# Second-half query and key projections by seven block products each, in a two-layer fp32 decoder step

## The chip, the cores and the metric

The kernel runs on one core of one Trainium2 chip. The metric is the device time of one execution in microseconds. All arithmetic is fp32. Engines are named as in the profile: PE is TensorE's matmul, PEld its load of stationary operands, DVE VectorE, ACT ScalarE, POOL GpSimd, SP the queue that issues most loads.

## The reference

Two layers run over 512 prompt tokens and 8 sample tokens of width 1024. Cut to the part that matters:

```python
def project_mixers(h, w_in_l, pos):
    z = h @ w_in_l
    qa, ka, va, qi, ki, wi, qb, kb, vb, gb = jnp.split(z, splits, axis=-1)
    qa = rope(qa...); ka = rope(ka...); qi = rope(qi...); ki = rope(ki...)
    qb = rope(qb.reshape(B, T, H_B, HEAD_DIM), pos)
    kb = rope(kb.reshape(B, T, H_B, HEAD_DIM), pos) * (HEAD_DIM ** -0.5)

def trunk_layer(x, l, pos, ...):
    h = rmsnorm(x, g_mix_pre[l])
    qa, ka, va, qi, ki, wi, qb, kb, vb, gb = project_mixers(h, w_in[l], pos)
    a = mixer_a(qa, ka, va, qi, ki, wi)                       # top-k sparse softmax attention
    b, S = retention_mixer(qb, kb, vb, gb, s0, g_ret_l)       # "second half"
    x = x + rmsnorm(concat([a, b]) @ w_out[l], g_mix_post[l])
    f = square(relu(rmsnorm(x, g_ffn_pre[l]) @ w_up[l])) @ w_down[l]
    x = x + rmsnorm(f, g_ffn_post[l])
    return x, ka, va, ki, S
```

## The kernel before

The engines run programs written out by hand, one instruction stream each, that meet at semaphores; each engine works strictly in the order of its stream. A layer is a chain of stages on PE. The input projection is cut into eight chunks of 512 columns: chunk 0 the indexer, 1 and 2 query and key of the first half, 3 its values, 4 and 5 query and key of the second half (qb, kb), 6 the gate, 7 the values of the second half. Then come 16 output products and the feed-forward part, whose large products already use seven block products for eight (`product`, L1063).

`project` (L702) makes one chunk: for each of four tiles of 128 tokens, eight matmuls (k = 0 to 7) with a 128x128 block of tokens as the stationary and 512 columns of weights as the moving operand, and a fifth tile for the 8 sample tokens (L724, 32 small matmuls). An fp32 matmul is two instructions in the trace. After each k a hook, `between`, may place other work. Two PSUM banks alternate from tile to tile, so a tile can start when the tile two before it has been read (`bank_taken`). ACT reads a finished tile, scaled by a per-token factor, into one of three buffers `raw` (`evacuate`, L1224), and DVE applies the rotary embedding from there into `zr` (`rope`, L1614 to L1620, four instructions).

Under chunks 4, 5 and 6 the sparse attention of 32 (query block, head) pairs runs as a pipeline of steps. `head_steps` (L90) spreads steps 0 to 35 over the tiles by their cost. Step i of `attend` is, on PE, for even i the scores of pairs i and i+1 (L863), for i of 3 and more the transposes of the probabilities of pair i-3 (L873), and for odd i of 5 and more the products with the values of pairs i-5 and i-4 (L850), placed before the transposes. On DVE it is for even i two `masked_max` (L1657 adds the mask and takes the maximum, L1660 multiplies it by -1/8), then for pair i-1 the reciprocal of the sum (L1672) and the scaling of the probabilities by it (L1675). On ACT it is the copy of the transposed pair i-3 (L1259) and the exponential of pair i (L1264). A pair is 128 to 512 wide, by query block. Between the steps DVE has ropes and, in chunk 6, the gate's `sigmoid` (L1684, two reciprocals L1688, L1692), which waits for ACT's exponential of the gate (L1232). At the end of a query block ACT also copies its output (`block_out`, L1271). At the start of chunk 4 PE also replicates the sample's values (L887) and transposes its probabilities (L893), and multiplies these with cached values in two groups (L905); the buffers of the second group's cache are those that earlier products have to be through with.

POOL has next to nothing to do from the copies of the new sample keys (L2167, chunk 3) to the gate's gains (L2173, chunk 6).

## Time and profile before

| | us |
|---|---|
| median of three runs | 1585.12 |
| lowest and highest | 1582.35, 1586.71 |
| the profiled execution's own time | 1587.15 |
| its span | 1585.4 |
| busy PE / DVE / ACT / POOL | 1559.8 / 829.9 / 440.6 / 419.4 |
| granted PE clock, mean share of full | 0.999 |

The two layers are nearly alike; chunk 4 of the first starts at 139.3 us and its chunk 6 ends at 281 us, and the second layer's are some 787 us later. A timeline row gives the start of a run of like instructions and its length up to the modelled end of the last, which overlaps the next row; so what a run costs is the distance from its start to the next start.

### The profile page before, as it was taken

To read this page: it belongs to the slowest core of one execution; us is meant where nothing else is said; L and a number is where in the kernel's file an instruction comes from. 1 tells how busy PE (TensorE), PEld (TensorE's weight loads), DVE (VectorE), ACT (ScalarE), POOL (GpSimd) and SP (SyncE) were. 2 spreads that over 40 slices of the span, in tenths; PEclk is the share of its full clock that TensorE was granted. 3 is DMA by queue.
4 is the path that set the end of the run, shared out by engine and by line. 5 is a ranking of instruction groups with operands and counts; after the bars stand their busy time and mean duration, and the time that the engine had idled before them with its cause. 6 is when DMAs were issued, how large, how long until landed. Compare 5 with 4: busy or idle time off the path is not lost.

```text
span 1585.4 us, 21168 instructions
## 1 busy us (share of the span) xinstructions
PE 1559.8 (98%) x7774; PEld 1117.7 (70%) x7774; DVE 829.9 (52%) x1752; ACT 440.6 (28%) x1021; POOL 419.4 (26%) x330
## 2 busy tenths in 40 slices
PE   8999999999999999999999999999999999999998
PEld 5444445588888888888844444456888888888887
DVE  4699567855653003332467985688466520133334
ACT  5222245224421002310252213452253310032101
POOL 0000001013654324444320000010236534233461
PEclk9999999999999999999999999999999999999999
DMA  6426310123331222212223262110233321222211
GB/s 209 132 69 214 133 54 11 45 85 107 133 133 54 107 103 84 80 57 103 87 78 107 80 222 99 54 54 3 84 134 133 107 106 54 106 96 91 80 53 54
DMA packets 52807, 150.35 MB, mean 95 GB/s; under 512 B 8250, under 2 KB 29506, under 8 KB 39394
## 3 DMA queue, kind: packets, MB, share of 16 engines
q1 hardware_dynamic: 45218, 140.65, 25.6%
q10 hardware_dynamic: 7488, 8.36, 1.6%
q8 instruction: 62, 1.02, 0.2%
q14 instruction: 39, 0.32, 0.1%
HBM read 139.79 MB, written 9.02 MB: 94 GB/s over the span
## 4 chain that ended last, share of the span: by engine, by line
PE 81%; DVE 12%; ACT 2%; DMA 2%; SPq 1%; issue 1%; POOL 1%; DVEq 0%; ACTq 0%; POOLq 0%
PE ps L1063 46%; PE ps L720 17%; PE ps L1001 7%; DVE arena L1643 2%; DVE top L1641 2%; PE ps L873 2%; PE ps L863 1%; PE ps L850 1%; DVE x_feat L1798 1%; PE ps L724 1%; PE ps L959 1%; DVE arena L1875 1%; DVE s_sb L1796 1%; ACT arena L1224 1%; DMA arena<-in_cache_v 1%
## 5 line engine op out<-in xcount | busy, mean ns | idle before, releaser
L720 PE MATMUL ps<-wring,h_feat 128*128 128x512 f32 (+1 forms) x960 | 436.0, 591 | 3.9 <-ACT h_feat L1186 2.3
L720 PEld LDWEIGHTS ps<-wring,h_feat 128*128 128x128 f32 x960 | 171.1, 191 | 176.2 <-issue 161.1
L1063 PE MATMUL ps<-arena,wring 128*128 128x256 f32 (+1 forms) x1280 | 285.8, 382 | 0.3 <-DVE arena L1882 0.3
L1063 PEld LDWEIGHTS ps<-arena,wring 128*128 128x128 f32 x1280 | 243.0, 190 | 37.7 <-DVE arena L1882 1.1
L1063 PE MATMUL ps<-h_feat,wring 128*128 128x256 f32 (+1 forms) x768 | 176.6, 381 | 0.0
L2149 POOL TENSOR_TENSOR wring<-wring,arena 128x512 f32<-128x512 f32 (+1 forms) x48 | 78.8, 1642 | 345.1 <-PE ps L1063 321.8
L1063 PEld LDWEIGHTS ps<-h_feat,wring 128*128 128x128 f32 x768 | 145.9, 190 | 21.6
L1063 PE MATMUL ps<-mix,wring 128*128 128x256 f32 (+1 forms) x512 | 120.2, 383 | 0.7 <-DVE p_sb L1856 0.7
L1063 PE MATMUL ps<-arena 128*128 128x264 f32 x512 | 119.2, 386 | 0.0
L1001 PE MATMUL ps<-mix,wring 128*128 128x256 f32 (+1 forms) x512 | 115.0, 383 | 0.8 <-ACT mix L1285 0.8
L1224 ACT ACTIVATE arena<-ps,rtok 128x512 f32<-128x512 f32 (+3 forms) x128 | 65.5, 512 | 174.0 <-PE ps L720 165.3
L1063 PEld LDWEIGHTS ps<-arena 128*128 128x128 f32 x512 | 97.3, 190 | 16.4
L1063 PEld LDWEIGHTS ps<-mix,wring 128*128 128x128 f32 x512 | 97.2, 190 | 16.2 <-DVE p_sb L1856 1.1
L1001 PEld LDWEIGHTS ps<-mix,wring 128*128 128x128 f32 x512 | 96.5, 190 | 15.5 <-issue 1.2
L2132 POOL TENSOR_TENSOR pt_sb<-pt_sb 128x256 f32<-128x256 f32 (+1 forms) x94 | 72.9, 776 | 126.2 <-ACT pt_sb L1160 122.7
L2173 POOL TENSOR_TENSOR arena<-arena,gret 128x512 f32<-128x512 f32 (+1 forms) x10 | 14.6, 1460 | 289.2 <-ACT arena L1232 289.2
L1326 ACT ACTIVATE arena<-arena 128x264 f32<-128x264 f32 (+1 forms) x96 | 40.4, 421 | 182.1 <-DVE arena L1882 131.6
L2149 POOL TENSOR_TENSOR arena<-wring 128x512 f32<-128x512 f32 (+1 forms) x48 | 79.4, 1655 | 35.0 <-DMA wring<-in_w_all 12.1
L2149 POOL TENSOR_TENSOR wring<-wring 128x512 f32<-128x512 f32 (+1 forms) x48 | 79.7, 1661 | 3.8
L2149 POOL TENSOR_TENSOR arena<-arena,wring 128x512 f32<-128x512 f32 (+1 forms) x48 | 79.3, 1653 | 3.8
L2167 POOL COPY arena<-kTs 128x4 f32<-128x4 f32 x16 | 3.5, 218 | 228.3 <-ACT kTs L1386 219.5
L1063 PE MATMUL ps<-mix,arena 128*128 128x264 f32 x256 | 62.2, 386 | 0.0
(225 smaller groups left out, 1804.6 us busy)
## 6 DMA issues: line engine op xcount, KB each, us to landing
wring<-in_w_all SPq DMA_DIRECT2D x108, 1024.0 KB, 5.0
arena<-in_cache_k SPq DMA_DIRECT2D x32, 256.0 KB, 5.2
arena<-in_cache_v SPq DMA_DIRECT2D x32, 256.0 KB, 4.3
o_k_out<-arena ACTq DMA_DIRECT2D x2, 1024.0 KB
o_v_out<-arena ACTq DMA_DIRECT2D x2, 1024.0 KB
arena<-in_state SPq DMA_DIRECT2D x2, 1024.0 KB, 4.8
o_rets_out<-arena ACTq DMA_DIRECT2D x2, 1024.0 KB, 9.5
wring<-in_w_idx SPq DMA_DIRECT2D x3, 648.0 KB, 5.7
```

The costliest lines, as they stand in the source:

```text
L720: last = mm(ps[:, proj_bank(n), 0:width], h_feat[:, k, token_cols(t)], wt, start=(k == 0), stop=(k == KD - 1))
L724: last = mm(ps[32 * g:32 * g + NB, proj_bank(n), 0:c1 - c0], h_feat[:, k, SEQ:TOK], wt[:, c0:c1], start=(k == 0), stop=(k == KD - 1))
L850: last = mm(ps[e * HD:(e + 1) * HD, 6 + b % 2, (h // 2) * P:(h // 2 + 1) * P], v_tok[:, m, (h + e) * HD:(h + e + 1) * HD], pt_sb[e][:, m * ...
L873: last = nc.tensor.transpose(ps[:, 2 + j % 2, m * P:(m + 1) * P], p_sb[j % P_SLOTS][:, m * P:(m + 1) * P], idn[:])
L1001: last = mm(ps[:, item_bank(n), 0:span(h)], wring[u % SLOTS][:, (m % 2 * KD + k) * P:(m % 2 * KD + k + 1) * P], mix[:, k, HALVES[h]], star ...
L1063: last = mm(out, a[:, j, :], b, start=(opens(n) and j == 0), stop=(j == nk - 1), skip_group_check=True)
L1224: nc.scalar.activation(dst[:, c0:c1], ps[rr, proj_bank(n), 0:c1 - c0], ACT.Copy, scale=rtok[rr, sc, t:t + 1]).then_inc(done, 1)
L1326: nc.scalar.activation(f, f, ACT.Relu).then_inc(act_step, 1)
L1641: v.max(t8, w).then_inc(dve_step, 1)
L1643: v.match_replace(w, t8, w, MARK).then_inc(dve_step, 1)
L2132: nc.gpsimd.tensor_tensor(ssum[:, hc], ssum[:, hc], sqr[added % 2][:, 0:span(h)], ALU.add).then_inc(sq_used, 1)
L2149: nc.gpsimd.tensor_tensor(dst, in0, in1, op).then_inc(s_ready, 1)
```

## The change

Chunks 4 and 5 (`BLOCKED`) are no longer made by tiles. Tokens, input features and output columns are each halved; the eight block products that this gives (256 tokens, 512 features, 256 columns each) become seven, numbered 1 to 7, of sums and differences of blocks. `project_blocks` runs them in the order 1, sample tile (0), 2, 6, 5, 7, 3, 4 (`BLOCKS`). One block product is eight matmuls with 256 moving columns, four for each of two token tiles. Products 2, 7 and 3 accumulate into the bank that 1, 6 and 5 left, once these have been read out.

POOL makes the operands: per layer four sums of token blocks (`input_sum`) and four sums of weight blocks per chunk (`chunk_sum`), each 128x1024: the token sums 1 to 3, chunk 4's sums 1 and 2, token sum 4, the other sums of chunk 4, and chunk 5's. ACT reads product 1 (`take_p1`) and 5 (`take_p5`) unscaled, product 2's bank scaled (`take_first`, two instructions of 256), and scales the other three quarters in SBUF once DVE has summed them (`scale_quad`, two instructions each). DVE adds five sums of 512 per chunk (`chunk_u2`, `_u3`, `_c22`, `_c12`, `_c21`); its ropes then work in place and follow later: four of chunk 5's five now stand in chunk 6.

Apart from that, the scaling of all 32 pairs' probabilities moves from DVE to ACT (in step i, the exponential of pair i and then the scaling of pair i-1, which waits for DVE's reciprocal), and `masked_max` takes the minimum of values already multiplied by -1/8, so that L1660 goes. `head_steps` spreads the steps by the new costs: steps 0 to 3 stand in products 3 and 4 of chunk 4, 4 and 5 in product 1 of chunk 5, 6 at the end of its sample tile, 7 and 8 in product 2, 9 and 10 in 6, 11 and 12 in 5, 13 and 14 in 7, 15 and 16 in 3, 17 and 18 in 4, then four to each tile of chunk 6 after k = 1, 3, 5, 7 (19 to 34), and 35 in its sample tile. Before, chunk 6 began with step 20 and its second tile with step 24.

The diff, cut to its core:

```diff
 FT = 16
-ATT_FROM = 4 * TILES + 3
+BLOCKED = (4, 5)
+BLOCKS = (1, 0, 2, 6, 5, 7, 3, 4)
 ATT_STEPS = NT * NH + 4
...
+            def project_blocks(c, between):
+
+                q = BLOCKED.index(c)
+                for i, n in enumerate(BLOCKS):
+                    if i < 2:
+                        unit_here(2 * c + i)
+                    taken, value = bank_taken(c, i)
+                    pe.wait_ge(taken, past(taken) + value)
+                    if n == 6:
+                        pe.wait_ge(chunk_sums, past(chunk_sums) + 4 * q + 2)
+                        pe.wait_ge(in_sums, past(in_sums) + 2)
+                    if n == 7:
+                        pe.wait_ge(chunk_sums, past(chunk_sums) + 4 * q + 3)
+                        pe.wait_ge(in_sums, past(in_sums) + 3)
+                    if n == 3:
+                        pe.wait_ge(chunk_sums, past(chunk_sums) + 4 * q + 4)
+                    if n == 4:
+                        pe.wait_ge(in_sums, past(in_sums) + 4)
+                    for k in range(KD):
+                        t, j = divmod(k, 4)
+                        low, high = slice(t * P, (t + 1) * P), slice((t + 2) * P, (t + 3) * P)
+                        if n == 0:
+                            last = sample_tile(c, i, k)
+                        else:
+                            a = {1: chunk_block(c, "11"), 2: chunk_block(c, "12"), 3: chunk_block(c, "12"),
+                                 4: chunk_block(c, "22"), 5: cs1, 6: cs2, 7: chunk_block(c, "21")}[n][:, j, :]
+                            b = {1: h_feat[:, j, low], 2: h_feat[:, 4 + j, low], 3: h_feat[:, 4 + j, high], 4: in4[:, j, low],
+                                 5: in1[:, j, low], 6: in2[:, j, low], 7: in3[:, j, low]}[n]
+                            last = mm(product_bank(c, n)[:, t, :], b, a, start=(opens(n) and k == 0), stop=(j == 3),
+                                      skip_group_check=True)
...
+            def take_p1(c):
+
+                if c == 5:
+                    act.wait_ge(out_k, past(out_k) + 32)
+                act.wait_ge(proj_done, past(proj_done) + product_at(c, 1))
+                nc.scalar.activation(quad_of(c, "21"), product_bank(c, 1), ACT.Copy).then_inc(proj_p1, 1)
+                act.wait_ge(proj_p1, up(proj_p1))
...
+            def take_first(c):
+
+                act.wait_ge(proj_done, past(proj_done) + product_at(c, 2))
+                scaled(c, "11", product_bank(c, 2), proj_c11)
+
+            def scale_quad(c, which, summed):
+
+                act.wait_ge(summed, past(summed) + BLOCKED.index(c) + 1)
+                scaled(c, which, quad_of(c, which), proj_scaled)
...
+            def beside(c, i):
+
+                if (c, i) == (4, 7):
+                    scale_quad(4, "22", proj_c22)
+                if (c, i) == (5, 0):
+                    scale_quad(4, "12", proj_c12)
+                if (c, i) == (5, 1):
+                    take_p1(5)
+                    act.wait_ge(as_mm, past(as_mm) + 1)
+                    nc.scalar.activation(mix[:, 0:4, SEQ:TOK], ps[:, 7, 0:4 * NB].rearrange("p (h b) -> p h b", b=NB), ACT.Copy).then_inc(as_read, 1)
+                    act.wait_ge(as_read, up(as_read))
+                    scale_quad(4, "21", proj_c21)
+                if (c, i) == (5, 2):
+                    evacuate(5, 1)
+                if (c, i) == (5, 3):
+                    take_first(5)
+                if (c, i) == (5, 5):
+                    take_p5(5)
+                if (c, i) == (5, 7):
+                    scale_quad(5, "22", proj_c22)
+                if (c, i) == (6, 0):
+                    scale_quad(5, "12", proj_c12)
+                if (c, i) == (6, 1):
+                    evacuate(6, 0)
+                    scale_quad(5, "21", proj_c21)
+                if c == 6 and i > 1:
+                    evacuate(6, i - 1)
...
                     act.wait_ge(att_read, past(att_read) + i + 1)
                     nc.scalar.activation(p_sb[i % P_SLOTS][:, 0:n], s_sb[i % 2][:, 0:n], ACT.Exp,
-                                         bias=neg_mx[:, i % 2:i % 2 + 1], scale=ATT_SCALE,
+                                         bias=neg_mx[:, i % 2:i % 2 + 1], scale=-1.0,
                                          accum_out=rsum[:, i % P_SLOTS:i % P_SLOTS + 1]).then_inc(p_exp, 1)
                     act.wait_ge(p_exp, up(p_exp))
+                if 1 <= i <= NT * NH:
+                    j = i - 1
+                    p = p_sb[j % P_SLOTS][:, 0:(j // NH + 1) * P]
+                    act.wait_ge(r_ready, past(r_ready) + j + 1)
+                    nc.scalar.activation(p, p, ACT.Copy, scale=rinv[:, j % 2:j % 2 + 1]).then_inc(p_ready, 1)
+                    act.wait_ge(p_ready, up(p_ready))
...
                 v.tensor_tensor_reduce(out=s_sb[c][:, 0:n], in0=ps[:, 4 + c, 0:n], in1=masks[b],
-                                       scale=1.0, scalar=-3e38, op0=ALU.add, op1=ALU.max, accum_out=mx[:, c:c + 1]).then_inc(dve_step, 1)
-                dve.wait_ge(dve_step, up(dve_step))
-                v.tensor_scalar(neg_mx[:, c:c + 1], mx[:, c:c + 1], -ATT_SCALE, None, ALU.mult).then_inc(att_read, 1)
+                                       scale=-ATT_SCALE, scalar=3e38, op0=ALU.add, op1=ALU.min,
+                                       accum_out=neg_mx[:, c:c + 1]).then_inc(att_read, 1)
...
-                    n, c = (j // NH + 1) * P, j % 2
                     dve.wait_ge(p_exp, past(p_exp) + j + 1)
-                    v.reciprocal(rinv[:, c:c + 1], rsum[:, j % P_SLOTS:j % P_SLOTS + 1]).then_inc(dve_step, 1)
-                    dve.wait_ge(dve_step, up(dve_step))
-                    p = p_sb[j % P_SLOTS][:, 0:n]
-                    v.tensor_scalar(p, p, rinv[:, c:c + 1], None, ALU.mult).then_inc(p_ready, 1)
-                    dve.wait_ge(p_ready, up(p_ready))
+                    v.reciprocal(rinv[:, j % 2:j % 2 + 1], rsum[:, j % P_SLOTS:j % P_SLOTS + 1]).then_inc(r_ready, 1)
+                    dve.wait_ge(r_ready, up(r_ready))
...
+            def chunk_u2(c):
+
+                dve.wait_ge(proj_p1, past(proj_p1) + BLOCKED.index(c) + 1)
+                dve.wait_ge(proj_done, past(proj_done) + product_at(c, 6))
+                v.tensor_tensor(quad_of(c, "12"), product_bank(c, 6), quad_of(c, "21"), ALU.add).then_inc(proj_u2, 1)
+                dve.wait_ge(proj_u2, up(proj_u2))
...
+            def beside(c, i, s):
+
+                if (c, i, s) == (4, 7, 0):
+                    chunk_c12(4)
+                if (c, i, s) == (5, 0, 0):
+                    chunk_c21(4)
+                if (c, i, s) == (5, 0, 1):
+                    rope(4, 2)
+                if (c, i, s) == (5, 2, 0):
+                    rope(4, 3)
+                if (c, i, s) == (5, 2, 1):
+                    rope(4, 0)
+                if (c, i, s) == (5, 3, 0):
+                    rope(4, 1)
+                if (c, i, s) == (5, 4, 0):
+                    chunk_u2(5)
+                if (c, i, s) == (5, 5, 0):
+                    rope(4, NT)
+                if (c, i, s) == (5, 6, 0):
+                    chunk_u3(5)
+                    chunk_c22(5)
+                if (c, i, s) == (5, 7, 0):
+                    chunk_c12(5)
+                if (c, i) == (6, 0):
+                    if s == 0:
+                        chunk_c21(5)
+                        rope(5, NT)
+                    if s in (1, 2):
+                        rope(5, 1 + s)
+                if c == 6 and i and s < 3:
+                    sigmoid(i - 1, s)
+                if (c, i, s) == (6, 1, 0):
+                    rope(5, 0)
+                if (c, i, s) == (6, 1, 3):
+                    rope(5, 1)
 
...
+            def input_sum(n):
+
...
+                    if now[0]:
+                        pool.wait_ge(h_ready, past(h_ready))
+                    else:
...
+                b21, b22 = h_feat[:, 4:8, low], h_feat[:, 4:8, high]
+                dst, in0, in1_ = {1: (in1, b12, b11), 2: (in2, b22, in1), 3: (in3, b22, b12), 4: (in4, in2, b21)}[n]
+                nc.gpsimd.tensor_tensor(dst, in0, in1_, ALU.subtract).then_inc(in_sums, 1)
+                pool.wait_ge(in_sums, up(in_sums))
+
+            def chunk_sum(c, n):
+
+                q = BLOCKED.index(c)
+                if n == 1:
+                    for u in (2 * c, 2 * c + 1):
+                        pool.wait_ge(w_slot[u % SLOTS], past(w_slot[u % SLOTS]) + 16 * (u // SLOTS + (u % SLOTS >= 2)))
+                    if q:
+                        pool.wait_ge(proj_done, past(proj_done) + product_at(BLOCKED[q - 1], 5))
+                    else:
+                        pool.wait_ge(dot_mm, past(dot_mm) + 3 * NI)
+                if n == 3:
+                    pool.wait_ge(proj_done, past(proj_done) + product_at(c, 0))
+                if n == 4:
+                    pool.wait_ge(proj_done, past(proj_done) + product_at(c, 2))
+                a11, a12, a21, a22 = (chunk_block(c, which) for which in ("11", "12", "21", "22"))
+                dst, in0, in1_, op = {1: (cs1, a21, a22, ALU.add), 2: (cs2, cs1, a11, ALU.subtract),
+                                      3: (a21, a11, a21, ALU.subtract), 4: (a12, a12, cs2, ALU.subtract)}[n]
+                nc.gpsimd.tensor_tensor(dst, in0, in1_, op).then_inc(chunk_sums, 1)
+                pool.wait_ge(chunk_sums, up(chunk_sums))
```

Three places show what the orders become; names before and after an arrow are what is written and read, and the brackets name the semaphores waited for.

PE, from the sums over the sample's heads (L918, now L1038) to the next work of chunk 5. Before:

```order
L918 MATMUL ps<-sel,arena 128x8 [waits om_ready]
L918 MATMUL ps<-sel,arena 128x8 x7
L720 MATMUL ps<-wring,h_feat 128x512 [waits proj_read]
L863 MATMUL ps<-arena 128x256 [waits att_read]
L863 MATMUL ps<-arena 128x256
L873 MATMUL ps<-idn,p_sb 128x128 [waits pt_ready,p_ready]
L720 MATMUL ps<-wring,h_feat 128x512 x3
```

Now:

```order
L1038 MATMUL ps<-sel,arena 128x8 [waits om_ready]
L1038 MATMUL ps<-sel,arena 128x8 x7
L785 MATMUL ps<-wring,h_feat 8x128 [waits proj_c21,w_slot3]
L785 MATMUL ps<-wring,h_feat 8x128 x31
L983 MATMUL ps<-arena 128x128 [waits att_read]
L983 MATMUL ps<-arena 128x128
L993 MATMUL ps<-idn,p_more 128x128 [waits pt_ready,p_ready]
L844 MATMUL ps<-wring,h_feat 128x256 [waits proj_p1]
L844 MATMUL ps<-wring,h_feat 128x256 x3
```

Before, the scores of a step (L863) stood inside a tile. Now the scores of step 6 (L983) and its transpose (L993) stand behind the whole sample tile (L785), and directly behind them product 2 (L844) waits for `proj_p1`, ACT's read of product 1.

ACT, at the same place: copy of transposes (L1259, now L1441), exponential (L1264, now L1446), scaling (L1454), and the reads of projections. Before:

```order
L1259 ACTIVATE pt_sb<-ps 128x128 [waits pv_mm,pt_mm,p_exp]
L1264 ACTIVATE p_sb,rsum<-s_sb,neg_mx 128x256 [waits att_read,pt_ready]
L1224 ACTIVATE arena<-ps,rtok 128x512 [waits rope_done,proj_done,p_exp]
L1418 ACTIVATE mix<-ps 128x4x8 [waits as_mm,proj_read]
L1259 ACTIVATE pt_sb<-ps 128x128 [waits pv_mm,pt_mm,as_read]
```

Now (from step 6 on):

```order
L1441 ACTIVATE pt_sb<-ps 128x128 [waits pv_mm,pt_mm,p_ready]
L1446 ACTIVATE p_more,rsum<-s_sb,neg_mx 128x128 [waits att_read,pt_ready]
L1454 ACTIVATE p_sb<-p_sb,rinv 128x128 [waits r_ready,p_exp]
L1360 ACTIVATE arena<-ps 128x2x256 [waits proj_done,out_k,p_ready]
L1398 ACTIVATE mix<-ps 128x4x8 [waits as_mm,proj_p1]
L1375 ACTIVATE arena<-arena,rtok 128x256 [waits proj_c21,as_read]
L1375 ACTIVATE arena<-arena,rtok 128x256 [waits act_step]
```

The read of product 1 (L1360) comes behind the copy, the exponential and the scaling of step 6.

DVE, in chunk 6 where the first gate tile's sigmoid starts (L1684 and L1688, now L1906 and L1910). Before:

```order
L1660 TENSOR_SCALAR neg_mx<-mx 128x1 [waits dve_step]
L1657 ISA s_sb,mx<-ps,arena 128x512 [waits p_exp,att_mm,att_read]
L1657 ISA mx 128x1
L1660 TENSOR_SCALAR neg_mx<-mx 128x1 [waits dve_step]
L1672 RECIPROCAL rinv<-rsum 128x1 [waits p_exp,att_read]
L1675 TENSOR_SCALAR p_more<-p_more,rinv 128x384 [waits dve_step]
L1684 TENSOR_SCALAR arena<-arena 128x512 [waits gate_exp,p_ready]
L1688 RECIPROCAL arena<-arena 128x256 [waits dve_step]
L1672 RECIPROCAL rinv<-rsum 128x1 [waits p_exp,dve_step]
L1675 TENSOR_SCALAR p_sb<-p_sb,rinv 128x512 [waits dve_step]
L1688 RECIPROCAL arena<-arena 128x256 [waits p_ready]
```

Now:

```order
L1897 RECIPROCAL rinv<-rsum 128x1 [waits p_exp,r_ready]
L1906 TENSOR_SCALAR arena<-arena 128x512 [waits gate_exp,r_ready]
L1910 RECIPROCAL arena<-arena 128x256 [waits dve_step]
L1810 TENSOR_TENSOR rstd_ffn<-arena,sinT 128x8x32 [waits proj_scaled,dve_step]
L1812 TENSOR_TENSOR rstd_ffn<-arena,sinT 128x8x32 [waits dve_step]
L1814 TENSOR_TENSOR arena<-arena,cosT 128x512 [waits dve_step]
L1816 TENSOR_TENSOR arena<-arena,rstd_ffn 128x512 [waits dve_step]
L1884 ISA s_sb,neg_mx<-ps,arena 128x512 [waits p_exp,att_mm,rope_done]
L1884 ISA neg_mx 128x1
L1884 ISA s_sb,neg_mx<-ps,arena 128x512 [waits p_exp,att_mm,att_read]
L1884 ISA neg_mx 128x1
L1897 RECIPROCAL rinv<-rsum 128x1 [waits p_exp,att_read]
```

Before, the two maxima of step 24 (L1657) came first and the sigmoid behind them. Now the sigmoid's first half and a rope (L1810 to L1816) stand between step 23's reciprocal (L1897) and step 24's maxima (L1884).

## Rows read from the trace of the kernel before

**Rows 1.** The page, part 1: busy time of each engine, share, instructions.
```profile
PE 1559.8 (98%) x7774; PEld 1117.7 (70%) x7774; DVE 829.9 (52%) x1752; ACT 440.6 (28%) x1021; POOL 419.4 (26%) x330
```

**Rows 2.** What TensorE waited for: us in total, times, longest us.
```profile
PE ps L905 <- DMA arena<-in_cache_v: 3.3, 2, 1.7
```

**Rows 3.** Busy time in a window (134 us): engines, TensorE clock, DMA.
```profile
145.00:279.00 134.00, 131.83 (x788) 62.46 (x788) 92.37 (x244) 55.35 (x135) 6.75 (x5) 1.00 0.25 91
```

**Rows 4.** Timeline of TensorE: start us, length us, instructions; 512 columns, then 256.
```profile
149.38 7.03 PE L720 MATMUL ps<-wring,h_feat 128*128 128x512 f32 x16
156.35 1.92 PE L905 MATMUL ps<-arena 128*32 128x512 f32 x16
...
337.61 10.53 PE L1001 MATMUL ps<-mix,wring 128*128 128x256 f32 x48
347.97 0.60 PE L970 MATMUL ps<-idn,arena 128*128 128x128 f32 x4
```

**Rows 5.** Timeline of TensorE: second sample value products and the wait for the cache.
```profile
158.20 7.13 PE L720 MATMUL ps<-wring,h_feat 128*128 128x512 f32 x16
166.96 1.93 PE L905 MATMUL ps<-arena 128*32 128x512 f32 x16 [1.62 <-DMA arena<-in_cache_v]
```

**Rows 6.** Timeline, TensorE: first pair of scores.
```profile
171.58 0.49 PE L863 MATMUL ps<-arena 64*128 64x128 f32 x4
```

**Rows 7.** Timeline, VectorE: the maximum of that score and its negation.
```profile
172.22 0.29 DVE L1657 CUSTOM_DVE_ANT_0 s_sb<-ps,causal_bias 128x128 f32<-128x128 f32 x1 [1.70 <-PE ps L863]
...
172.56 0.15 DVE L1660 TENSOR_SCALAR neg_mx<-mx 128x1 f32<-128x1 f32 x1
```

**Rows 8.** Timeline, ScalarE: the exponential of that score.
```profile
172.80 0.40 ACT L1264 ACTIVATE p_sb<-s_sb,neg_mx 128x128 f32<-128x128 f32 x1 [15.61 <-DVE neg_mx L1660]
```

**Rows 9.** Groups by form, 145 to 280 us: busy us, mean ns, idle before.
```profile
L1688 DVE RECIPROCAL arena<-arena 128x256 f32<-128x256 f32 x8 | 14.0, 1753 | 0.3
...
L1224 ACT ACTIVATE arena<-ps,rtok 128x512 f32<-128x512 f32 x12 | 8.3, 688 | 7.0 <-PE ps L720 6.7
...
L1614 DVE TENSOR_TENSOR arena<-arena,cosT 128x512 f32<-128x512 f32 x8 | 5.5, 692 | 5.9 <-ACT arena L1224 5.8
...
L1224 ACT ACTIVATE arena<-ps,rtok 8x128 f32<-8x128 f32 x13 | 4.7, 360 | 0.4
...
L1259 ACT ACTIVATE pt_sb<-ps 128x384 f32<-128x384 f32 x8 | 3.9, 491 | 10.9 <-issue 6.9 <-PE ps L873 4.0
...
L1616 DVE TENSOR_TENSOR rstd_ffn<-arena,sinT 128x256 f32<-128x256 f32 x8 | 3.4, 424 | 0.3
...
L1264 ACT ACTIVATION_READ_ACCUMULATOR p_sb<-s_sb,neg_mx 128x1 f32 x16 | 3.0, 186 | 0.0
...
L1264 ACT ACTIVATE p_sb<-s_sb,neg_mx 128x512 f32<-128x512 f32 x4 | 2.9, 722 | 2.2 <-DVE neg_mx L1660 2.1
...
L1232 ACT ACTIVATE arena<-arena 128x512 f32<-128x512 f32 x4 | 2.5, 630 | 0.1
...
L1259 ACT ACTIVATE pt_sb<-ps 128x128 f32<-128x128 f32 x8 | 2.2, 278 | 6.0 <-issue 4.2 <-PE ps L873 1.6
...
L1675 DVE TENSOR_SCALAR p_more<-p_more,rinv 128x512 f32<-128x512 f32 x4 | 1.9, 486 | 0.1
```

**Rows 10.** Timeline, TensorE: scores of steps 24 and 26.
```profile
239.84 1.13 PE L863 MATMUL ps<-arena 64*128 64x512 f32 x4
...
246.10 1.13 PE L863 MATMUL ps<-arena 64*128 64x512 f32 x4
```

**Rows 11.** Timeline, ScalarE: a copy of transposed probabilities late in chunk 6.
```profile
255.25 0.60 ACT L1259 ACTIVATE pt_sb<-ps 128x512 f32<-128x512 f32 x1
```

**Rows 12.** Timeline, TensorE: the values product that reads such copies.
```profile
256.69 1.09 PE L850 MATMUL ps<-pt_sb,arena 128*64 128x128 f32 x16
```

**Rows 13.** Groups by form, GpSimd: busy us, mean ns, idle before.
```profile
L2149 POOL TENSOR_TENSOR wring<-wring 128x1024 f32<-128x1024 f32 x16 | 38.2, 2389 | 1.3
```

**Rows 14.** Timeline, GpSimd: its last work before the gate.
```profile
127.36 1.15 POOL L2167 COPY arena<-kTs 128x4 f32<-128x4 f32 x4 [4.03 <-PE ps L832]
```

More of the change, by code:

```diff
@@ new lines, in take_p5, with scaled @@
+            def take_p5(c):
+                act.wait_ge(proj_done, past(proj_done) + product_at(c, 5))
+                nc.scalar.activation(quad_of(c, "22"), product_bank(c, 5), ACT.Copy).then_inc(proj_p5, 1)
+                act.wait_ge(proj_p5, up(proj_p5))
+            def scaled(c, which, src, done):
+                a, b = int(which[0]) - 1, int(which[1]) - 1
+                for e in range(2):
+                    t = 2 * b + e
+                    sm = done if e else act_step
+                    nc.scalar.activation(quad_of(c, which)[:, e, :], src[:, e, :], ACT.Copy,
+                                         scale=rtok[:, 1 if c == 5 else 0, t:t + 1]).then_inc(sm, 1)
+                    act.wait_ge(sm, up(sm))
```

258 lines of the change are left out of this document (176 added, 82 removed).

## Prediction

> **What bounds the kernel.** I read the page first: PE is busy 98% of the span, DVE 52%, ACT 28%, POOL 26% [rows 1]. The list of PE's waits comes next. Its longest entry under chunks 4 to 6 is 1.7 us, for the cache of sample values, once per layer [rows 2]. The window from 145 to 279 us, the most of chunks 4 to 6 of the first layer, has PE at 131.8 of 134 us, at full clock (2.4 GHz), DVE at 92.4, ACT at 55.4 [rows 3]. So what PE has to issue sets the time here, and the others come early enough. The question is whether they still do when PE needs less and ACT does more.
>
> **What PE saves.** Sixteen instructions of 512 columns take 156.35 - 149.38 = 6.97 us, 0.436 each; inside a tile they come closer, at 0.427 (512 columns in two passes at full clock would be that). Forty-eight of 256 take 347.97 - 337.61 = 10.36 us, 0.216 each [rows 4]. A chunk's four tiles were 64 instructions, 27.3 to 27.9 us. Seven products are 112 instructions, 112 x 0.216 = 24.2 us. That is 3.1 to 3.7 us less per chunk; I take 3.4, as some tiles are cut up by steps and some are not. Four chunks: **-13.7 us**. Sample tiles, steps and their number stay.
>
> **POOL's sums: nothing.** Twelve of 128x1024 per layer at 2.39 us [rows 13]. The first five are due when product 6 of chunk 4 starts, some 12 us after that chunk's start at 139.3, and POOL is free from 128.5 [rows 14]: 5 x 2.4 = 12 us, done at about 141. Product 7 needs a sum that starts after the sample tile, product 3 one that starts after product 2, each one to two products (3.4 us each) ahead. Cover is 5 us or more; half as long again would still be hidden.
>
> **DVE: relieved, but no gain by itself.** Each of 32 pairs loses the negation (0.15 [rows 7]) and the scaling (0.49 at 512 [rows 9]), some 17 us a layer; ten sums of about 0.69 come in. DVE was not on the path.
>
> **ACT: the added work.** No row shows a scaling of probabilities on ACT. The read of a projection with a per-token factor has the same form: 0.36 for 128 columns, 0.69 for 512 [rows 9]. The bounds are the plain copy below (0.28 and 0.60 [rows 9, 11]) and the exponential with its sum above (0.72 + 0.19 at 512 [rows 9]); I take 0.36, 0.47, 0.58 and 0.69 for the four widths, 17 us a layer. Reading products 1, 5 and 2 and scaling three quarters adds about 4 more than the four tile reads that go, so ACT comes to about 55 + 17 + 4 = 76 us of some 134. Its share is harmless. Its place is not: before, a pair's scaling hung on DVE alone, which did it after its own maxima. Now it hangs on DVE's reciprocal and stands behind the next pair's exponential, and PE's transposes hang on it.
>
> The Trainium skill, ScalarE: Activation LUTs, section on rules for kernel authors, says to put a multiplication on VectorE rather than ScalarE. The rows agree in size (0.49 against 0.69); by the rule the move alone costs at most the difference, 0.1 to 0.2 x 64 pairs, about 9 us, if all of it stood in PE's path, and nothing where it does not.
>
> **The new waits, each per layer.** A hand-over from DVE to ACT takes 0.09 us (172.71 to 172.80 [rows 7, 8]), to PE about 0.15.
>
> (a) *Cache of the second sample group: +0.25.* Loads start when the first products are through; before, PE came back 7.1 us later and waited 1.62 [rows 5]. Now two block products, 6.9 us, lie between.
>
> (b) *Product 2 of chunk 5: +2.25.* It waits for ACT's read of product 1, which stands behind step 6, whose scores PE issues right before. From their start: 0.64 to DVE's maximum [rows 6, 7], 0.34 for it, ACT's exponential from about 1.15 on (its copy comes before) for 0.5 [rows 8], scaling 0.36, read of 512 columns 0.60, gaps and hand-over 0.2: 2.8. PE itself needs 0.58 for scores and transpose.
>
> (c) *Product 6 of chunk 5: +0.55*, on the sample tile's read behind step 7. From product 2's start: 1.8 of matmuls, transposes visible to ACT at 2.6 (an estimate with the same 0.6), copy 0.31, exponential 0.5, scaling 0.39, four reads of 0.36 with gaps 1.54: 5.5 with the hand-over. PE is there at 4.97. *Product 5 of chunk 5: +0.25*, likewise on the read of product 2 behind step 9.
>
> (d) *Step 26's scores: +1.75.* In chunk 6 the sigmoid's first part and a rope now stand before the maxima of step 24. From PE's start of step 23: its transposes reach ACT after 1.4 (an estimate: three quarters of the values product's 1.09 [rows 12], and 0.6 on the way as in rows 6 and 7); copy 0.49, exponential of 384 0.8, scaling 0.58, gate's read 0.69, gate's exponential 0.63 with gaps: 4.8. Then DVE: addition 0.45 (an estimate by the scaling's 0.49), reciprocal 1.75, rope 2 x 0.69 + 2 x 0.42 with gaps 2.37 [rows 9], two maxima of 512, 1.46: 11.0 with the hand-over. From the scores of step 24 to those of 26 PE took 246.10 - 239.84 = 6.26 us [rows 10], so three steps are about 9.25.
>
> (e) *Behind it: +0.35, +1.4, +0.5.* The products of step 27 wait for a copy that stands behind scaling 24. Those of step 29 wait for the copy of pair 25: DVE does a second rope and the decayed keys before reciprocal 26, ACT's scaling 26, the second gate tile (0.69 + 0.63) and a block's output (0.60) come before that copy. Before, that copy ended 0.84 ahead of the products that need it (255.25 + 0.60 = 255.85 and 256.69 [rows 11, 12]); it now has a rope and a scaling, 3 us, more ahead. Step 33's wait 0.5 behind the third gate tile.
>
> Sum per layer: 0.25 + 2.25 + 0.55 + 0.25 + 1.75 + 0.35 + 1.4 + 0.5 = 7.3 us, twice **+14.6 us**. Chunk 7, where DVE is busiest, should start as before: by the same reckoning DVE begins the fourth sigmoid no later against PE. The sum is -13.7 + 14.6 = +0.9 us against the profiled execution's own 1587.15. That one lies 2.0 above the median of the three, so the forecast is 1585.1 + 0.9 = **1586.0 us**. A measurement of this kernel can tell 0.3%, 4.8 us, from no change.
>
> **Rivals.**
> *The waits don't come, the saving stays (faster).* For it: ACT is idle more than half the stage [rows 3], and only (b) follows from the order alone. Against: chains of five and more instructions in (d) and (e) have no idle time in them. If (d) and (e) vanish and the rest stands: 2 x 4.0 less, 1578 us; with all waits gone 1571.4.
> *ACT paces the end of chunk 6 (slower).* If a scaling costs as much as the exponential with its sum (0.94 instead of 0.72 with gaps), the chain of every one of the last 12 steps, which is full, gets 0.22 longer, and with (b) and (c) three more: 2 x 15 x 0.22 = 6.6, with the waits of steps that now just make it (14, 15, 31), 0.2 each, about 8 us: 1594. It decides from a scaling of about 0.9 at 512.
> *The product count is not what PE pays.* A block product's instruction has half the columns over which the next stationary load must be hidden. If it doesn't fit, each 0.01 us over 0.216 costs 448 x 0.01 = 4.5 us. Against it: the 48 instructions of rows 4 load one each and keep 0.216.
>
> **Numbers.** My forecast, all waits within a third of their size (5 us in the total either side): 0.45. Faster through missing waits: 0.28, of it 0.05 for all gone. ACT as the pace, or waits that I have not seen: 0.27. From these: faster by over 0.3% 0.3, within 0.3% 0.4, slower 0.3. The sign of the likeliest case is open; its own range is 1581 to 1591. The range for 8 in 10 reaches to the two other cases without their ends, 1576 to 1596.
>
> **What would show it.** In the changed trace: (1) block products at 0.216 us an instruction, 24.2 us per chunk without waits; (2) a wait of about 2.2 us of product 2 on the read of product 1 in chunk 5, once per layer, the longest one; (3) scalings on ACT at 0.36 to 0.69; (4) in chunk 6 scores of step 26 that wait for DVE's maxima by 1.5 to 2 us, and products of step 29 that wait for ACT's copy by about 1.4; (5) POOL done with each sum before PE asks; (6) chunk 7 as long as before. The forecast is wrong if (2) and (4) are missing, which gives the faster case, or if PE waits in most steps of chunk 6, which gives the slower one. The probabilities' path would then be what I misread, not the matmuls.

## The result and the profile after

The change makes the kernel 0.8% slower: 1597.49 us, median of four runs (1594.93 to 1598.03), against 1585.64 (four runs) of the kernel before. The ratio is 1.0079, 95% interval 1.0067 to 1.0091. The forecast was 1586.0 in 1576 to 1596, with 0.3 on slower. The profiled execution took 1598.03 us, its span is 1596.3, its mean granted clock 0.993 (before 0.999). Two runs that lie far off, one of experiment 6 (5691.69 us) and one of the kernel before beside experiments 9 to 12 (1804.6 us), count in no ratio.

The page's first part, busy time by engine, answers rows 1:

```profile
PE 1555.8 (97%) x7966; PEld 1159.2 (73%) x7966; DVE 814.3 (51%) x1644; ACT 488.0 (31%) x1109; POOL 475.1 (30%) x354
```

PE is busy only 4 us less, where 13.7 us of work were to go; stretches at the low clock, shown below, make up for most of it. What it waited for (us in all, times, longest us) answers rows 2:

```profile
PE ps L1025 <- DMA arena<-in_cache_v: 4.5, 2, 2.6
PE ps L785 <- ACT arena L1346: 4.1, 2, 2.3
PE ps L844 <- ACT arena L1360: 4.0, 2, 2.0
PE ps L970 <- ACT pt_sb L1441: 3.9, 6, 1.2
PE ps L983 <- DVE neg_mx L1884: 3.0, 2, 1.5
...
PE ps L857 <- ACT arena L1428: 1.0, 2, 0.6
...
PE ps L844 <- ACT arena L1346: 0.6, 2, 0.3
```

L1025 is the products with the cached values, L785 the sample tile, L844 a block product, L970 the products with the values, L983 the scores. The cache (L1025), product 2 (L844 behind L1360), L970 and L983 were forecast in kind, and, but for the cache, in size. L785 was not: the sample tile of chunk 4 waits for ACT's read of chunk 3's last tile.

The timeline of PE (start, length, instructions, idle time before) shows the waits and a slower PE behind some of them. First layer, cached values and product 2 of chunk 5:

```profile
156.37 1.92 PE L1025 MATMUL ps<-arena 128*32 128x512 f32 x16
158.23 3.72 PE L844 MATMUL ps<-arena 128*128 128x256 f32 x16
161.78 3.62 PE L844 MATMUL ps<-wring,mix 128*128 128x256 f32 x16
168.04 3.50 PE L1025 MATMUL ps<-arena 128*32 128x512 f32 x16 [2.64 <-DMA arena<-in_cache_v]
171.47 1.99 PE L844 MATMUL ps<-wring,h_feat 128*128 128x256 f32 x8
...
191.03 3.12 PE L844 MATMUL ps<-wring,h_feat 128*128 128x256 f32 x8 [2.01 <-ACT arena L1360]
194.09 0.70 PE L970 MATMUL ps<-pt_sb,arena 128*64 128x128 f32 x4
```

Sixteen instructions with the cache took 1.92 us at 156.4 and 3.50 at 168.0; eight of a block product took 3.12 at 191.0 where 1.99 is usual. The windows say why (busy time by engine; the number behind the counts is the granted TensorE clock, then DMA):

```profile
162.00:167.00 5.00, 3.40 (x16) 2.66 (x14) 1.46 (x2) 0.60 (x1) 4.70 (x2) 1.00 0.90 301
167.00:172.00 5.00, 3.96 (x18) 1.17 (x19) 0.71 (x2) 0.00 (x0) 0.00 (x0) 0.66 0.03 11
172.00:182.00 10.00, 10.00 (x52) 7.83 (x50) 3.55 (x14) 4.50 (x14) 0.00 (x0) 1.00 0.41 128
...
190.00:195.00 5.00, 3.97 (x14) 2.61 (x15) 2.90 (x5) 2.17 (x5) 0.86 (x1) 0.67 0.00 0
...
937.00:947.00 10.00, 10.00 (x43) 5.80 (x37) 5.78 (x12) 2.76 (x7) 2.34 (x1) 0.55 0.77 299
...
982.00:988.00 6.00, 4.20 (x14) 3.04 (x15) 3.35 (x8) 2.87 (x8) 1.63 (x1) 0.72 0.00 0
```

Behind four of the six long waits of chunks 4 and 5 PE worked at the lower level, 1.2 GHz, for about 3 to 10 us at a time. Against the same instructions at 2.4 GHz that costs 1.57 us at 168.0, 1.48 from 191.0 on, 4.9 from 935.1 to 946.2, and 1.58 at 983.8: 9.5 us. The kernel before has one such stretch in its profile, in chunk 4 of the second layer, worth 1.7. No long wait stands before it: the last one is 1.03 us, at 923.5, and the fall comes at 934:

```profile
930.00:935.00 5.00, 4.88 (x10) 1.57 (x9) 4.69 (x12) 1.93 (x5) 0.00 (x0) 0.90 1.03 363
935.00:940.00 5.00, 5.00 (x13) 2.67 (x12) 4.76 (x12) 1.28 (x2) 0.00 (x0) 0.76 1.01 407
```

**The account**, from the two profiled executions, whose spans lie 10.9 us apart: matmuls saved -13.7 (see the last part); forecast waits (cache +1.2, product 2 4.0, product 6 0.6, chunk 6 6.9) +12.7; the sample tile's wait less the 0.5 that stood there before, +3.6; low clock +7.8 (9.5 less 1.7); chunk 7's transposes wait 1.7 less (L857's line against one of 2.7 us, four times, before); the feed-forward part (0.8) and the cached keys (0.3) wait 1.1 more; a wait for weights at 28.0 us, 1.1 before, is gone, -1.1. Sum +8.7; 2.2 us of the difference have no term. From the start of chunk 4 to that of chunk 7 PE takes 4.0 us more in the first layer and 5.8 more in the second, so about 9.9 of the 10.9 arise there.

Chunk 6 of the first layer went as forecast; the sigmoid and a rope on DVE stand ahead of the maxima of step 24:

```profile
243.99 0.43 DVE L1906 TENSOR_SCALAR arena<-arena 128x512 f32<-128x512 f32 x1 [4.88 <-ACT arena L1352]
244.46 1.75 DVE L1910 RECIPROCAL arena<-arena 128x256 f32<-128x256 f32 x1
246.24 0.42 DVE L1810 TENSOR_TENSOR rstd_ffn<-arena,sinT 128x256 f32<-128x256 f32 x1
...
248.61 0.69 DVE L1884 CUSTOM_DVE_ANT_0 s_sb<-ps,arena 128x512 f32<-128x512 f32 x1
```

and PE's scores of step 26 and the products of step 29 wait for it:

```profile
250.10 1.13 PE L983 MATMUL ps<-arena 64*128 64x512 f32 x4 [1.48 <-DVE neg_mx L1884]
...
261.43 1.09 PE L970 MATMUL ps<-pt_sb,arena 128*64 128x128 f32 x16 [1.22 <-ACT pt_sb L1441]
```

DVE had 4.88 us without work right before, so the wait looks like one of order, not of load; experiment 8 tests this.

### The profile page after: what moved, and what is told of

It reads as the page before. It is cut to its first block, busy times and chain, and to the rows that moved or that the text cites. A ratio compares the mean times of both kernels' runs of the same rounds, so it can differ in the third digit from the quotient of the medians.

```text
span 1596.3 us, 21682 instructions
## 1 busy us (share of the span) xinstructions
PE 1555.8 (97%) x7966; PEld 1159.2 (73%) x7966; DVE 814.3 (51%) x1644; ACT 488.0 (31%) x1109; POOL 475.1 (30%) x354
## 4 chain that ended last, share of the span: by engine, by line
PE 79%; DVE 13%; ACT 3%; issue 2%; DMA 1%; SPq 1%; POOL 1%; ACTq 0%; DVEq 0%; POOLq 0%
PE ps L1183 45%; PE ps L807 10%; PE ps L1121 7%; PE ps L844 5%; DVE arena L1870 2%; DVE top L1868 2%; PE ps L785 1%; PE ps L772 1%; PE ps L970 1%; PE ps L993 1%; PE ps L983 1%; DVE x_feat L2020 1%; PE ps L1079 1%; ACT arena L1346 1%; DVE arena L1816 1%
## 5 line engine op out<-in xcount | busy, mean ns | idle before, releaser
L807 PE MATMUL ps<-wring,h_feat 128*128 128x512 f32 (+1 forms) x704 | 316.0, 586 | 3.0 <-ACT h_feat L1306 2.2
L807 PEld LDWEIGHTS ps<-wring,h_feat 128*128 128x128 f32 x704 | 124.7, 190 | 125.5 <-issue 112.5
L1346 ACT ACTIVATE arena<-ps,rtok 8x128 f32<-8x128 f32 (+3 forms) x112 | 54.7, 488 | 157.0 <-PE ps L807 148.7
L1491 ACT ACTIVATE p1s<-ps 128x256 f32<-128x256 f32 x40 | 15.4, 385 | 162.2 <-PE ps L1183 162.1
L1183 PE MATMUL ps<-h_feat,arena 128*128 128x264 f32 x256 | 62.2, 386 | 0.0
```

Source lines behind the costliest of these rows:

```text
L807: last = mm(ps[:, bank_of(c, i), 0:width], h_feat[:, k, token_cols(t)], wt, start=(k == 0), stop=(k == KD - 1))
L1183: last = mm(out, a[:, j, :], b, start=(opens(n) and j == 0), stop=(j == nk - 1), skip_group_check=True)
L1346: nc.scalar.activation(dst[:, c0:c1], ps[rr, bank_of(c, i), 0:c1 - c0], ACT.Copy, scale=rtok[rr, sc, t:t + 1]).then_inc(done, 1)
```

## The experiments

All are timed against the kernel before on the same chip (its median there 1585.1 to 1585.2). Intervals are of the ratio.

**1. The attention part alone**, on the kernel before: minimum, and scalings on ACT.

```diff
-                       scale=1.0, scalar=-3e38, op0=ALU.add, op1=ALU.max, accum_out=mx[:, c:c + 1])
-                v.tensor_scalar(neg_mx[:, c:c + 1], mx[:, c:c + 1], -ATT_SCALE, ...)
+                       scale=-ATT_SCALE, scalar=3e38, op0=ALU.add, op1=ALU.min, accum_out=neg_mx[:, c:c + 1])
-                    v.tensor_scalar(p, p, rinv[:, c:c + 1], None, ALU.mult)      # on DVE
+                    nc.scalar.activation(p, p, ACT.Copy, scale=rinv[...])        # on ACT, behind the exponential
```

> The kernel before with the attention part of the change alone: minimum in place of the negated maximum, scalings of probabilities on ScalarE, no block products. Theory A (the loss of the change, 1597.5 against 1585.6, comes from waits of TensorE around the block products and from the TensorE clock that falls after them): this kernel takes 1583 to 1588, granted clock 1.00 as before, no wait over 1 us in chunks 5 and 6. Theory B (ACT paces the probabilities' path, the moved scalings are the loss): 1592 or more, with waits of the transposes or values products on ACT in chunk 6.

Measured 1586.73 (1.0008, 0.9999 to 1.0016), clock 0.998 to 1.000: no difference. In the kernel before, the moved scalings cost nothing, and theory B falls.

**2. The block products alone**: experiment 1's edit the other way, on the changed kernel.

> The changed kernel with the attention part put back (maximum, negation and scalings on DVE), block products alone. Theory A: the waits of the sample tile (4.1 us in all), of the cache of values (4.5) and of product 2 of chunk 5 (4.0, about 0.7 less without the scaling) stay and so does the fallen clock: 1593 to 1600. DVE then has rope, sigmoid and scalings together in chunk 6, so waits there may be longer. Theory B: the loss goes, 1583 to 1587.

Measured 1589.56 (1.0034, 1.0015 to 1.0052), runs from 1584.7 to 1597.9 at clocks from 1.000 down to 0.994. It is slower than before, as A says, but less so than its 1593 to 1600, which was reckoned from 1597.5. The spread was not expected either; in the main the slower runs are those with the lower clock. DVE's maxima are late by 6.0 us in all.

**3 and 4. One wait taken away each**, in the changed kernel: ACT reads chunk 3's last tile before two exponentials for which it has to wait; ACT reads product 1 of chunk 5 ahead of step 6.

```diff
+                evacuate(3, 4)
                 for g in range(2):
                     act.wait_ge(smx_ready, past(smx_ready) + g + 1)
...
-                evacuate(3, 4)
```
```diff
+                        if (c, i, s) == (5, 1, 0):
+                            take_p1(5)
                         attend(step)
...
                 if (c, i) == (5, 1):
-                    take_p1(5)
```

> The changed kernel; on ACT the read of chunk 3's last tile is moved ahead of the two exponentials of the sample scores. Theory A: the sample tile of chunk 4 no longer waits (1.8 us in layer 1, 2.3 in layer 2), and in layer 2 the slow stretch right behind that wait (about 4.2 us lost in the products of the sample values and block product 2) goes with it: 1597.5 - 4.1 - 4.2 = about 1589. Theory C (the wait only hides behind the next one, since the cache of values comes at a time of its own): the wait for the cache grows by as much, 1596 to 1598. Theory D (the slow clock is not tied to the wait): 1593.5.

Measured 1587.35 (1.0010, 1.0001 to 1.0019), clock 0.995 to 0.999. The sample tile's wait is gone, the cache's is 4.9 (4.5 in the changed kernel's first profile). The clock still falls behind the cache's wait of 2.96 and behind both waits of product 2.

> The changed kernel; in chunk 5 ACT reads product 1 ahead of step 6 instead of behind it. Theory A: product 2 of chunk 5 no longer waits (2.0 us in each layer) and the slow stretch behind the wait (1.5 us in layer 1, 1.7 in layer 2) goes with it: 1597.5 - 4.0 - 3.2 = about 1590. Theory C (something else is late right behind: step 6's transposed copy or the sum that opens product 6): at most 1 us is gained, 1596.5. Theory D (the slow clock is not tied to the wait): 1593.5.

Measured 1584.75 (1.0006, 0.9994 to 1.0018), from 1581.6 at 0.999 to 1592.4 at 0.995. In its profiled execution the clock did not fall in chunks 4 to 6, though the sample tile waited 1.4 and 1.9 us; it fell once elsewhere, near 799 us, in the second layer's first chunk. Against the first runs of the changed kernel, 1597.5, each gained more than twice its wait. But those are runs of another time; against experiment 5, the changed kernel again on another chip, experiment 3 gains 3.4 us and experiment 4 6.0.

**5. The changed kernel again.**

> The changed kernel as it is, beside the others of this group on one chip, to see whether its time and granted clock (1597.5, 0.993) belong to the kernel. Theory A (waits and the fallen clock behind them are the kernel's): 1594 to 1599, clock 0.992 to 0.995. Theory E (the low clock came with the chip or the hour): 1585 to 1590 at 0.998 or more.

Measured 1590.76 (1.0043, 1.0023 to 1.0062), runs from 1586.6 at 0.998 to 1601.2 at 0.989. Neither A nor E as put: it is slower than before here too, but the clock falls in some executions more than in others, and the runs lie 14.6 us apart. The waits in its profile are those of the first (sample tile 3.9, cache 4.0, product 2 4.0); the clock fell behind two of the six (and once near 805 us, behind no long wait).

**6. Cached values one block product later** (`(5, KD - 1)` becomes `(6, KD - 1)` in `beside_qb`).

> The changed kernel; the products of the sample probabilities with the second group's cache of values stand one block product later (behind product 3 of chunk 4 instead of product 7). Theory A: the wait for the cache (2.6 and 1.9 us) goes, as that product takes 3.55 us, and so does the slow stretch behind it in layer 1 (1.6 us); DVE's maxima of steps 0 and 1 stand behind those products' sums, which makes step 2's scores wait 0.3 twice: 1597.5 - 4.5 - 1.6 + 0.6 = about 1592. Theory C (the loads are late by more than the trace shows): 1596. Theory D (slow clock not tied to waits): 1593.6.

Measured 1588.89 (1.0021, 1.0008 to 1.0034). The cache's wait is gone, step 2's scores wait 0.47 twice for DVE. Product 2's wait stayed and both times the clock fell behind it. So 3.1 us of waits went, and the kernel is 1.9 us faster than in experiment 5, less than the spread of either (9 and 15 us): alone this move shows little.

**7. The three moves together.**

> The three moves together: early read of chunk 3's last tile, early read of product 1 of chunk 5, later products with the second group of cached values. Theory A: all three waits go (4.1 + 4.0 + 4.5 us) and the granted clock is back at 0.999 or more, which is worth 8 of the 9 us lost at 1.2 GHz: 1597.5 - 12.6 - 8.2 + 0.6 = about 1577, runs within 3 us of each other. Theory D: 1585.5 at a clock of 0.993 to 0.995.

Measured 1575.86 (0.9936, 0.9923 to 0.9949), five runs from 1574.2 to 1576.7, clocks 0.999 and 1.000. The largest waits left in chunks 4 to 6:

```profile
PE ps L983 <- DVE neg_mx L1885: 3.9, 4, 1.5
PE ps L970 <- ACT pt_sb L1440: 3.8, 6, 1.2
```

and the windows of chunks 4 and 5 of both layers, all at full clock:

```profile
139.00:180.00 41.00, 40.53 (x267) 30.00 (x266) 25.12 (x63) 15.79 (x41) 12.34 (x6) 1.00 0.71 255
180.00:225.00 45.00, 44.45 (x294) 29.53 (x294) 28.75 (x79) 30.84 (x78) 4.71 (x2) 1.00 0.14 50
925.00:966.00 41.00, 40.53 (x287) 30.00 (x286) 23.47 (x59) 15.47 (x42) 11.79 (x5) 1.00 0.61 225
966.00:1011.00 45.00, 44.45 (x238) 27.72 (x237) 29.30 (x80) 31.30 (x78) 2.35 (x1) 1.00 0.12 48
```

A holds: the waits are gone, the clock is back and the runs lie 2.5 us apart. The kernel takes 14.9 us less than the changed one on the same chip (experiment 5). The three waits were 11.9 us there, a new one of 0.9 comes in, and the other 3.9 are put down to the clock. A had 8.2 for the clock, as it was reckoned from the runs of 1597.5, which had lost more by it.

**8. A fourth move, in chunk 6.** ACT scales chunk 5's last quarter behind step 21, DVE does two ropes in its idle time, the first sigmoid a step later.

```diff
+                        if (c, i, s) == (6, 0, 2):
+                            scale_quad(5, "21", proj_c21)         # ACT; was behind evacuate(6, 0)
...
-                if c == 6 and i and s < 3:
+                if (c, i, s) == (6, 0, 3):
+                    rope(5, 1)
+                if (c, i, s) == (6, 1, 0):
+                    rope(5, 0)
+                if c == 6 and i == 1 and s:
+                    sigmoid(0, s - 1)
+                if c == 6 and i > 1 and s < 3:
                     sigmoid(i - 1, s)
```

> The three moves and a fourth, in chunk 6: ACT scales the last quarter of chunk 5's keys three steps earlier, DVE does the ropes of tiles 1 and 0 where it is idle (behind steps 22 and 23), the first tile's sigmoid a step later each. The forecast waits (d) and (e), measured as 1.5 + 0.2 + 1.2 + 0.5 us a layer, come from DVE's and ACT's order there: by this 4 to 5 of 6.9 us go, and the kernel takes 4.5 less than the one with three moves, about 1572.5. If the waits come from the sum of work in chunk 6 and not its order, it takes the same as with three.

Measured 1568.70 (0.9894, 0.9880 to 0.9908): order, not load. The gain is 7.2 us where 4.5 were expected; both lines together shrink from 7.7 to 1.8, and the other 1.3 have no term. What is left in chunk 6 is the 0.9 of L970; the 0.9 of L983 is step 2's:

```profile
PE ps L983 <- DVE neg_mx L1886: 0.9, 2, 0.5
PE ps L970 <- ACT pt_sb L1439: 0.9, 2, 0.5
```

**9. A longer wait in the kernel before.** Its products with the second group of cached values four steps k earlier.

```diff
-                if (i, k) in ((1, KD - 1), (2, KD - 1)):
+                if (i, k) in ((1, KD - 1), (2, 3)):
```

> The kernel before, without block products, with one thing changed: the products with the second group of cached values stand four matmuls (1.7 us) earlier, so that TensorE waits 3.3 us for the loads in each layer instead of 1.6 and does the four matmuls afterwards. Theory A (a wait of 2 us and more brings the clock down, in any kernel): 1585.1 + 3.4 = 1588.5 for the waits and 1.5 to 4 us more for the slow stretches, 1590 to 1592, clock 0.996 to 0.998 and runs that differ. Theory F (the block products bring it down, the wait alone does not): 1588.5 at 0.999.

Measured 1595.71 (1.0070, 1.0056 to 1.0084). The expectation counted a step k as one instruction; it is two, so the move is 3.5 us. The waits in the profile grew from 3.3 to 9.3 us, which alone gives about 1591 by both theories, and 1595.7 is 4.5 more. The clock decides: it is 0.995 to 0.997 in every run, where the kernel before beside it had 0.998 to 1.000, and the timeline shows the slow products behind both waits (3.54 and 3.64 us where 1.92 is usual), without a block product in the kernel:

```profile
157.70 1.92 PE L905 MATMUL ps<-arena 128*32 128x512 f32 x16
159.55 3.70 PE L720 MATMUL ps<-wring,h_feat 128*128 128x512 f32 x8
167.41 3.54 PE L905 MATMUL ps<-arena 128*32 128x512 f32 x16 [4.16 <-DMA arena<-in_cache_v]
...
958.54 3.64 PE L905 MATMUL ps<-arena 128*32 128x512 f32 x16 [5.16 <-DMA arena<-in_cache_v]
```

A third slow stretch of this run, from 146.8 to 150.7, stands behind a wait of 0.44 only; it is like the one in the second layer of the kernel before.

**10. The two moves that bear on it, in the kernel before** (early read of chunk 3's last tile, cached values at `(3, 3)`).

> The kernel before, without block products, with the two moves that bear on it: early read of chunk 3's last tile, and the products with the second group of cached values four matmuls later. It says how much of what the four moves gave would have come without the change. The wait for the cache (3.3 us in all) and the one for the sample values (0.5) go: about 1581.3. If the block products are what makes the four moves pay, this one stays more than 10 us above 1568.7.

Measured 1585.16 (1.0000, 0.9991 to 1.0009). The forecast of 1581.3 is missed: the 3.3 us of cache wait are gone, and step 3's transposes wait 2.9 instead, since the cached values now stand behind step 0's scores and DVE sums them before the maxima. So this order gives the kernel before nothing; it stays 16 us above experiment 8. Whether another order would speed up the kernel before is not tested.

**11. The four moves with the attention part on DVE.**

> Block products with the four moves, and the attention part put back (maximum, negation and scalings on DVE). Theory G (the scalings on ACT are a need of the block products, since DVE also does their sums and the late ropes in chunk 6): DVE's maxima are late there in two or more steps, 6 us of waits as in the kernel with block products alone against 1.8 us now: 1573 to 1575. Theory H (either engine has room once the order is right): 1567 to 1570.

Measured 1574.88 (0.9940, 0.9927 to 0.9954): theory G. DVE's maxima are late again, and block products wait for two of DVE's sums (L1818, L1836):

```profile
PE ps L982 <- DVE neg_mx L1882: 4.6, 6, 0.8
...
PE ps L969 <- ACT pt_sb L1438: 1.3, 2, 0.7
...
PE ps L843 <- DVE arena L1836: 1.0, 2, 0.5
...
PE ps L843 <- DVE arena L1818: 0.7, 2, 0.4
```

**12. Two moves more**: the sample tile of chunk 5 read ahead of step 7, the maxima of steps 0 and 1 ahead of the second half of the sample output.

> The four moves and two more: ACT reads chunk 5's sample tile ahead of step 7, and DVE does the maxima of steps 0 and 1 ahead of the second half of the sample output. The waits of product 6 (0.55 a layer) and of step 2's scores (0.47) go, 2 us in all: 1568.7 - 2.0 = about 1566.7. If what stands behind them is late too, 1568 to 1569.

Measured 1567.66 (0.9894, 0.9879 to 0.9909), within 1 us of experiment 8. The 0.47 of step 2 went; in place of product 6's 0.55 stands one of 0.7 for the read of product 2's bank, which the earlier read pushed back. With a ratio of 0.989 these two are the fastest found.

**Waits and clock in chunks 4 and 5, over all profiled executions.** A wait counts as followed by the low clock when the instructions right behind it took over 1.3 times as long as elsewhere.

| place (what PE did before) | waits, us | followed by 1.2 GHz |
|---|---|---|
| cached values (block products, or matmuls of 512 columns in the kernel before) | eleven of 1.11 to 1.99 | none but one of 1.99 |
| the same | 2.56, 2.64, 2.96, 4.16, 5.16 | all |
| product 2 of chunk 5 (3.6 us of small matmuls: 16 with 8 moving columns, 64 with 8 stationary ones) | 1.63, 1.63 and eight of 2.0 | one of 1.63, seven of 2.0 |
| sample tile of chunk 4 (block product 1) | ten of 1.41 to 2.31 | 2.12, 2.31 |

The length of the last wait is not the whole rule, and no experiment here finds the rest. Outside the table, the first wait of every kernel (4.7 to 4.9 us, for ACT at the start of the first layer) was never followed by 1.2 GHz, nor was any in chunk 6 (up to 1.72). One of 1.70 for the cached keys, with the sample tile's 64 small matmuls before it, was (experiment 11, second layer). And the clock also fell where PE had not waited long: in chunk 4 of the kernel before and of experiments 1 and 9, and near 800 us in experiments 3 to 6, behind waits of 0.2 to 0.7 us that experiment 7 has too, at full clock.

## Why the prediction was wrong

**The saving was right.** The prediction had 0.216 us an instruction and 27.3 to 27.9 a chunk before. Between waits eight instructions of chunk 5 take 1.82 to 1.85, 0.229 each, 25.6 us for 112, and the 64 they replace took 29.0. The two figures were about 5% low, and the difference, 3.4 a chunk, is the one taken: two errors of 1.4 us that cancel, which is luck (four times 3.4 is 13.6, not 13.7). The rival of the product count has no room: what the block products cost over 0.216 an instruction, the tiles had cost over 0.427 to 0.436. The sums on POOL cost nothing: each took 2.34 to 2.41 us, and PE never waited for one.

**(a)**, the cache, was +0.25 a layer; the waits grew by 1.0 and 0.2. In the first layer PE could go on 9.8 us after the first group's end, where it had been 8.8 [rows 5].

**(b)**, product 2 behind ACT's read: forecast 2.25, measured 2.01 in each layer. **(c)**, products 6 and 5: 0.55 and 0.25, measured 0.29 to 0.34 and nothing. **(d)**, step 26: 1.75, measured 1.48. **(e)**, what is behind it: 0.35, 1.4, 0.5, measured 0.24, 1.22, 0.49. A scaling took 0.40, 0.51, 0.62 and 0.73 us where 0.36 to 0.69 was taken. Experiment 8 shows that (d) and (e) hang on the order of DVE and ACT: with a new order and the same work 0.9 of their 6.8 us in two layers are left.

**The step that failed first** is the list of new waits itself. It follows every bank and read of chunk 5 and misses the sample tile of chunk 4, which comes 3.5 us sooner because one block product stands before it in place of a whole tile. Its bank is free when ACT has read chunk 3's last tile, and ACT does that behind a table load and two exponentials, for which it waits until 140.7:

```profile
140.75 1.28 ACT L1582 ACT_TABLE_LOAD   x1 [5.97 <-DVE nms L2239]
...
143.25 1.54 ACT L1346 ACTIVATE arena<-ps,rtok 8x128 f32<-8x128 f32 x4
```

and PE's sample tile, in the first and the second layer:

```profile
144.94 1.50 PE L785 MATMUL ps<-wring,h_feat 128*8 128x128 f32 x48 [1.77 <-ACT arena L1346]
...
935.12 2.12 PE L785 MATMUL ps<-wring,h_feat 128*8 128x128 f32 x48 [2.31 <-ACT arena L1346]
```

The trace of before had what was needed to see it. The same read ends at 143.56 + 1.54 = 145.10, and PE's replication of the sample's values already waited for it:

```profile
143.56 1.54 ACT L1224 ACTIVATE arena<-ps,rtok 8x128 f32<-8x128 f32 x4
```
```profile
145.25 1.95 PE L887 MATMUL ps<-arena,exps 8*128 8x512 f32 x4 [0.55 <-ACT arena L1224]
```

A block product that starts at 139.3 is through at about 142.9 (an estimate by its 16 instructions at 0.222), 2 us earlier. The waits cost 4.1 us, 3.6 more than before. Experiment 3 takes them away with one line moved, though 0.9 of them come back as wait for the cache (4.9 against experiment 5's 4.0). The chance of 0.27 had "waits that I have not seen" in it, but the sum had none.

**The step that failed most** is the price of a wait. The sum, and its range of "5 us in the total either side", count a wait at its length and let the work behind it run at full clock, as in the window of [rows 3]. The waits of 1.6 to 1.7 us before had cost no more than that. The change brings waits of 1.8 to 2.6 us, and behind four of six TensorE ran at 1.2 GHz: 7.8 us in the profiled execution. Experiments 7 and 9 show this from both sides: without the waits the block products run at 1.000, and the kernel before, with a wait of 4 to 5 us, runs at 0.996. Taken off the 10.9 us measured, the two errors (3.6 and 7.8) leave -0.5, where the forecast's sum was +0.9. The signs that the prediction named for being wrong did not show it: (2) and (4) came in kind and near their size, though (2) was not the longest wait (2.01 against 2.64 for the cache), and PE did not wait in most steps of chunk 6.

**Rivals.** "ACT paces the end of chunk 6" gave 1594, near the result, for a reason that does not hold: it asked for a scaling of about 0.9 at 512 columns, and 0.73 was measured; the moved scalings alone cost nothing (experiment 1), and the loss stays when they are put back on DVE (experiment 2). The Trainium skill, ScalarE: Activation LUTs, section on rules for kernel authors, puts a multiplication on VectorE rather than ScalarE. Here the row agrees in the price of one (0.73 against 0.49 at 512 columns), and the measurement goes the other way for the kernel: with block products and the four moves, the attention part as the change has it, with the scalings on ScalarE and no negation on VectorE, is 6.2 us faster (1568.7 against 1574.9). In the slower one TensorE waits for VectorE, which also has the sums and late ropes (experiment 11); what the negation's share is was not measured. "The waits don't come, the saving stays" gave 1571; experiments 8 and 12 reach it and go a little below, by order alone.

What stays open: why the clock falls behind some waits of 2.0 us and not behind others of the same place and length, and at times behind no long wait, so that the changed kernel's median was 1597.5 in one group of runs and 1590.8 in another.

## What to carry to other kernels

When a change shortens work ahead of a wait, list every hand-over in the stretch in front of which less work now stands, not only those that the change adds: here a tile that was not touched came 3.5 us early. In this kernel a wait of 2 us or more on TensorE often cost about as much again in low clock (1.5 to 4.9 us each), and the runs spread over 15 us instead of 3; so look at the granted clock before and after, and mend such waits first. And where an engine has idle time right ahead of a late result (4.9 us here), try another order before less work.

## What was not expected of the hardware

The low clock behind waits of about 2 us (table above), most often where small matmuls of 8 columns stood ahead of the wait (no experiment changed these alone); the same program at 0.989 in one execution and 0.998 in another, with run times 14.6 us apart in all (experiment 5); and eight loads of 256 KB for the cache, the last of which let PE go on between 7.9 (experiment 9) and 10.1 us (experiment 3) after the buffers came free, in kernels that ask for them in the same way.
